# Four small decay products issued one projection earlier, and a token shift moved behind four running sums

## The reference, cut to what matters

```
u = rmsnorm(h, norm1_g); proj = u @ w_in
p = proj_rwkv + (previous token - proj_rwkv) * mu      # token_shift
r, k, v, wd, ad, gd = split(p)                         # 512, 512, 512, 64, 64, 128 columns
w = -softplus(-(w0 + tanh(wd) @ w_decay_up)) - 0.5
a = sigmoid(a0 + ad @ a_up);  g = sigmoid(gd) @ g_up
kk = normalised(k * k_k);  k = k * (1 + (a - 1) * k_a)
decay = exp(-exp(w))
for each token t:                                      # state is 64x64 per head, 8 heads
    state = state * decay_t - (state kk_t) (kk_t a_t)^T + v_t k_t^T
    y_t = state r_t
```

## Time and profile before

| | us |
|---|---|
| median of 3 runs | 2115.5 (2113.46 to 2120.26) |
| the profiled execution's own time | 2115.5 |
| its span, first to last instruction | 2113.7 |
| PE busy | 1999.2 (95%) |
| DVE / ACT / POOL busy | 919.4 / 798.7 / 989.2 |
| mean granted TensorE clock | 0.978 of full speed |

### The profile page before, as it was taken

One profiled execution on the slowest core, in us unless ns is written; L12 is line 12 of the kernel. 1 busy time (PEld: TensorE's weight loads), 2 busy tenths in 40 slices (PEclk: granted clock), 3 DMA queues, 4 the chain that ended last, 5 costly groups with the idle time before them and its releaser, 6 DMA issues.

```text
span 2113.7 us, 26127 instructions
## 1 busy us (share of the span) xinstructions
PE 1999.2 (95%) x10110; PEld 1621.6 (77%) x10110; DVE 919.4 (43%) x1496; ACT 798.7 (38%) x1044; POOL 989.2 (47%) x766
## 2 busy tenths in 40 slices
PE   5998899998999999999999887989999999999997
PEld 3785796875778887888888666966987788888886
DVE  2679643776433034222200687456974541111101
ACT  3565224335554224322222643344325643222221
POOL 3635613564313464565556463004453265565662
PEclk9998999999999999999999999999999999999999
DMA  6311104721112331222223311012421222222222
GB/s 278 100 60 60 41 1 185 288 96 59 60 42 80 110 126 70 93 100 100 100 100 101 128 60 61 2 51 66 139 100 60 100 100 81 99 100 100 100 100 80
DMA packets 30826, 199.58 MB, mean 94 GB/s; under 512 B 5488, under 2 KB 7664, under 8 KB 9712
## 3 DMA queue, kind: packets, MB, share of 16 engines
q1 hardware_dynamic: 30704, 197.92, 26.0%
HBM read 188.99 MB, written 4.19 MB: 91 GB/s over the span
## 4 chain that ended last, share of the span: by engine, by line
PE 85%; DVE 7%; ACT 3%; DMA 2%; POOL 1%; issue 1%; SPq 0%; DVEq 0%; ACTq 0%; POOLq 0%
PE ps L418 23%; PE ps L419 23%; PE ps L420 23%; PE ps L478 2%; DMA ar<-ada_dram 2%; PE ps L830 1%; PE ps L843 1%; DVE ar L1883 1%; PE ps L508 1%; DVE ar L1909 1%; PE ps L899 1%; DVE ar L1982 1%; PE ps L612 1%; DMA raw<-panels_dram 1%; PE ps L835 1%
## 5 line engine op out<-in xcount | busy, mean ns | idle before, releaser
L2523 POOL TENSOR_TENSOR WL<-raw,WH 128x512 fp32r<-128x512 f32 x588 | 780.0, 1327 | 920.8 <-ACT WH L1305 884.9
L418 PE MATMUL ps<-hH,WH 128*128 128x512 f32 x1648 | 661.3, 401 | 27.0 <-DVE xL L1872 7.4
L420 PE MATMUL ps<-hH,WL 128*128 128x512 f32 x1648 | 647.8, 393 | 0.0
L419 PE MATMUL ps<-arR,WH 128*128 128x512 f32 x1392 | 542.5, 390 | 0.0
L1305 ACT CAST WH<-raw 128x2048 fp32r<-128x2048 f32 x147 | 280.9, 1911 | 507.1 <-DMA raw<-panels_dram 505.9
L418 PEld LDWEIGHTS ps<-hH,WH 128*128 128x128 f32 x1648 | 313.9, 190 | 107.6 <-issue 33.4
L420 PEld LDWEIGHTS ps<-hH,WL 128*128 128x128 f32 x1648 | 312.9, 190 | 67.1
L419 PE MATMUL ps<-xL,WH 128*128 128x512 f32 x848 | 335.5, 396 | 0.0
L419 PEld LDWEIGHTS ps<-arR,WH 128*128 128x128 f32 x1392 | 262.0, 188 | 54.3 <-issue 0.2
L418 PE MATMUL ps<-arR,WH 128*128 128x512 f32 x592 | 230.6, 390 | 0.0
L420 PE MATMUL ps<-arR,WL 128*128 128x512 f32 x592 | 230.3, 389 | 0.0
(11 more groups left out here) (384 smaller groups left out, 2217.4 us busy)
## 6 DMA issues: line engine op xcount, KB each, us to landing
raw<-panels_dram SPq DMA_DIRECT2D x145, 1024.0 KB, 4.8
ar<-ada_dram SPq DMA_DIRECT2D x12, 2048.0 KB, 11.9
xT<-xT_dram SPq DMA_DIRECT2D x2, 2048.0 KB, 8.6
out_dram<-xT SPq DMA_DIRECT2D x8, 512.0 KB, 2.7
ar<-ar SPq DMA_DIRECT2D x12, 256.0 KB, 6.9
xT<-out_dram SPq DMA_DIRECT2D x1, 2048.0 KB, 9.1
wide<-wide_dram SPq DMA_DIRECT2D x1, 1024.0 KB, 6.8
ar<-ar SPq DMA_DIRECT2D x8, 128.0 KB, 3.9
```

Of the source, the lines that this page charges most:

```text
L418: mm(out, lhs[0], rhs[0], start=first, stop=False)
L419: mm(out, lhs[0], rhs[1], start=False, stop=False)
L420: return mm(out, lhs[1], rhs[0], start=False, stop=final)
L2523: ins = tt(WL[:, n % SLOTS, c], raw[:, n % SLOTS, c], WH[:, n % SLOTS, c].bitcast(F32), ALU.subtract)
```

## The change

PE issues the four `wup` products directly behind `wag` 0 and `rkv` 4 instead of behind `rkv` 5; then `rkv` 5, the four `aup`, and `rkv` 6 and 7 together. DVE does `mix(2)`, the token shift of `rkv` 5, behind the four running sums instead of ahead of them. No instruction is added or removed on any engine, and none changes its shape.

```diff
                 project_by_k([("wag", 0), ("rkv", 4)], h_mix, lambda k: norm_step("low", "rms3", k))
-                project("rkv", h_mix, 1, i0=5)
                 pe.wait_ge(small2_in, 16)
                 pe.wait_ge(sem("lora_act"), 1)
                 for p in range(4):
                     begin("wup", p)
                     end(mm(pst("wup", p), lora[0:64, 0, p * P:(p + 1) * P], tile(WA)[0:64, :], start=True, stop=True))
-                project("rkv", h_mix, 1, i0=6)
+                project("rkv", h_mix, 1, i0=5)
                 for p in range(4):
                     begin("aup", p)
                     end(mm(pst("aup", p), lora[64:P, 0, p * P:(p + 1) * P], tile(WA)[64:P, :], start=True, stop=True))
-                project("rkv", h_mix, 1, i0=7)
+                project("rkv", h_mix, 2, i0=6)
...
                 mix(0)
                 mix(1)
-                mix(2)
                 for p in range(4):
                     emptied(dve, "wup", p)
                     link(v.tensor_tensor_scan(tile(40 + p), wide[:, 3, :], tile(LD + p), 0.0, ALU.mult, ALU.add))
                     link(tt(tile(LD + p), tile(40 + p), tile(LD + p), ALU.subtract), sem("g_cum"), p + 1)
+                mix(2)
                 mix(3)
```

## The result

The changed kernel takes 2130.4 us (median of 10 runs, 2120.4 to 2139.1) against 2119.1 us of the kernel before on the same chip (10 runs, 2113.5 to 2127.0). The ratio is 1.0051, 95% interval 1.0027 to 1.0076: slower by 0.5%, 11 us. A second set gave 1.0068, 1.0043 to 1.0093. The forecast was slower, 2122.8 us, range 2118 to 2126. Its sign held, and the time lies above its range.

What follows compares the result with a forecast made beforehand. Up to 1241 us DVE and what feeds it set the end, with PE 6.1 us to spare. From 2115.5: 0 (earlier `wup`) + 0 (PE's idle) + 7.3 (ACT held, sums and mix included) = 2122.8 us, range 2118 to 2126.

Steps and rivals of the forecast that it cites:

- No gain from the early `wup`: `wup` begins 2.3 us earlier on PE, but ACT's table load and first sigmoid stay put: gain 0.
- PE's new idle time: PE stands 3.1 us ahead of `wup`, is about 4.5 us behind at `rkv` 5, hidden by slack: cost 0.
- the term for the fallen clock: PE's low clock after the idle time ahead of `wup` costs 1.6 to 2 us; 1.6 used.
- the slack at the `rm` products: PE's 6.13 us wait for DVE at 1241 hides PE's delay if nothing else is late.
- Faster sums, 2.7 us: DVE's four running sums, no longer beside POOL's panel work, take 9.2 us instead of 11.94.
- ACT held in `key_parts(1)`: ACT's `key_parts(1)` waits for the moved `mix(2)` until 1211.8; clamps 6.0 to 7.8 us later, 7.3 taken at `rm`.
- the other way in: Through PE: `kkn` 3 waits for ACT's square, then `rkv` 1; `mix(6)` starts 6.1 to 7.7 us later.
- The prediction's own sign of being wrong: Wrong if the shift at line 898 is not the shift at the end within 1.5 us.
- The first: Rival: faster sums win, DVE's row -1.1 us and `rm` products earlier, 2114.4 us; chance 0.07.
- The second: Rival: half of the 7.3 us is made up in the later stretch to 1318, 2119 us; chance 0.18.
- The third: Rival: DVE slowed beside POOL throughout, `rkv` 1 at low clock, POOL beside the transposes, 2125.5 us; chance 0.13.
- The base: The sum starts from 2115.5 us, the profiled execution's time and also the median of the runs, unconverted.

Runs made afterwards that it cites:

- the first trace: First profile of the changed kernel, unaltered: 72.3 us from the first `wag` 0 matmul to the first `rm` product (the stretch), against 62.7 before.
- the third trace: Changed kernel profiled a third time, unaltered: stretch 70.2 us, against 62.7 in the trace of before with like `wag` 0 and `rkv` 4.
- D: Kernel before with PE's wait for the tanh ahead of `rkv` 5 instead of behind it: stretch 66.2 us against 62.7.
- C: Changed kernel with both 13 unused matmuls ahead of `wup` and `key_parts(1)` behind `decays(1)`: stretch 65.25 us, 1.0009 of before.
- A: Changed kernel with 13 unused matmuls filling PE's idle time ahead of `wup`: stretch 71.8 us, 1.0056 of before.
- B: Changed kernel with `key_parts(1)` moved on ACT behind `decays(1)`: stretch 72.2 us, 1.0075 of before.
- E: Both kernels unchanged, traced twice more each: stretches over three traces 62.7, 64.0, 64.0 us before and 72.3, 72.2, 70.2 after.
- F: Kernel before with ACT's `wup` sigmoids earlier, then `aup` sigmoids too: stretches 64.2 and 65.1 us; the second kernel 0.9992 of before.

## Why the prediction was wrong

*No gain from the early `wup`.* Right: the first running sum stayed behind ACT's load and sigmoid.

*PE's new idle time.* This is the step that failed. The prediction put PE "about 4.5 us" behind and had `rkv` 6 end "near 1214.4", 36 us into the stretch, with 6.13 us of slack to hide it. `rkv` 6 was done at 41.7 in the first trace and at 37.9 in the third. The idle time was right (3.07 against 3.1 us); the term for the fallen clock, 1.6 us, measured 3.5 on `wup` (7.16 against 3.70) and 2.6 on `rkv` 5 (8.2 us from the end of `wup` to `aup`, against 5.6), 6 us in all; in the third trace 2.1 and 1.1, 3.2 us. The rows it was taken from the earlier trace rows have 128-row matmuls behind the idle time, and the place at hand has 64-row ones; D with the third trace shows that this accounts for a part of the mis-sizing, 3.2 us against 1.7. What made it 6 in the other traces stays open. And the slack at the `rm` products was the wrong one to count: `mix(3)` needs `rkv` 6 long before, and behind it DVE has no slack.

*Faster sums, 2.7 us.* Right: 0.69 us for each of the last three subtractions, 9.1 us for the eight instructions. C shows that they bring nothing: what they win goes to `mix(2)` and to the wait for `rkv` 6.

*ACT held in `key_parts(1)`.* Right in place and wait (8.74 us against the "some 8.5" of the prediction). In the third trace of after, where it decided the end, the clamps started 55.0 us into the stretch instead of 47.5 and the stretch cost 7.5 us, nearly the 7.3 of the forecast. With the clock held up, in A, the clamps also started 7.4 us later (54.9 against 47.5 us into the stretch), inside the 6.0 to 7.8 forecast. But the other way in, `kkn` 3 and `rkv` 1, was 1.5 us longer than its range: PE stood 4.24 us there, not 2.6, and `kkn` 3 itself ran at the low clock, 2.04 us instead of 0.9. `mix(6)` came 9.2 us late, not 6.1 to 7.7.

*The sum.* Two delays lie side by side, and the later one counts: 8.3 us by PE's in two traces of three, 7.5 by ACT's in the third. Alone they measured 8.3 (B) and 9.1 (A). So the stretch explains 0.2 to 1.0 us of the 7.6 by which the forecast was low. The base gives 3.6 (2119.1 against 2115.5). And the sum let nothing be added behind the first `rm` product, where like traces differ by 1 to 3 us more. The rest is not assigned. The prediction's own sign of being wrong also came: the shift at line 898 was 4.6 us between the two first traces, and at the end 17.6. Most of that difference is chance: the traces of before differ among themselves by up to 12 us from the first `rm` product on, and the part ahead of the stretch moved every absolute time by 5.0.

*The rivals.* The first, a gain, would need PE's products on time and did not come even in C. The second, half given back later, is refuted for this change: behind the stretch the changed kernel was 1 to 3 us longer than the like traces of before, not shorter. The third had the low clock in it, but at `rkv` 1 (7.0 us instead of 5.4) and not at `wup` and `rkv` 5.

*The base.* The base was a median of 3 runs and one profiled execution, and that had the shortest parts of all three traces of before in E. It stood 2.5 us under the median of 23.

Open: the medians differ by 11 us in the first set and 17 in the second, like traces by 10. The lowest runs of the two kernels differ by 9 us (2111.6 and 2120.4), the highest by 9 (2131.9 and 2140.7), which fits the like traces. Whether the change also makes the later falls of the clock more frequent, three traces of each cannot tell. Nor is it shown how PE's idle time makes the piece behind the `rm` products 1.5 us longer.

## What to carry to other kernels

An instruction that fills an idle hole of its engine is free only until it is moved: first ask who waits for its result, and what stands behind that waiter. Where two waits grow at once, undoing one of them shows nothing; take away both, then each. Size a fall of PE's clock from a place with the same instructions behind the idle time, give it a range and not one value, and test it against the next consumer of PE, not against the last. And when single traces are compared, look first at a piece that the change does not touch: if its length differs, compare with another trace.

## What the runs showed of the hardware

Behind 3.07 us of idle time and eight passes over 64 rows first, PE was at 1.2 GHz for 12.1 us of unbroken work in the first trace of the changed kernel, and for 6.8 us in the third. Where matmuls over 128 rows came first behind the same 3.07 us, it was for 3.5 us (D). With such matmuls behind 4.75 us of idle time, ahead of `wag` 0, it was for 3.4 us in the first trace of before and 5.4 us in the first of after. The kernel before varied by 20 us from run to run (2111.6 to 2131.9), with a mean granted clock of 0.970 to 0.981: a wait of 1.84 us ahead of small products let the clock fall in two of its three traces and not in the other. A table load of ACT that came behind a wait for PE added its 1.28 us to that wait (F).

The Trainium skill, in "TensorE: Matmul & The Clock Gate", Part 1, says that how many matmuls run at the low clock at a kernel's start differs between runs of one kernel. These traces show such a difference in the middle of a kernel (`wup` at 7.16 and at 5.83 us in two traces of the changed kernel).
